# Expert up product: a 512-column and a 256-column matmul in place of three of 256, with the partial sums added outside TensorE

## The reference, cut to what matters

```
u = modulate(x, sh_ffn, sc_ffn)              # 256 x 1024
y = (gelu(u @ U.T) * G) @ V                  # 256 x 1024
x = layer_norm(DN_ALPHA * x + g_ffn * y, ln2_g, ln2_b)
```

## Time and profile before

| | |
|---|---|
| median of 3 runs | 4242.46 us (4237.34 to 4247.29) |
| the profiled execution | 4238.88 us, its span 4237.0 us |
| busy share | PE 81%, PEld 71%, DVE 63%, ACT 43%, POOL 2% |
| TensorE clock granted, mean | 0.908 of full |
| HBM | 633.89 MB read, 150 GB/s over the span |
| expert stages | 796 to 1553 us and 2316 to 3065 us of the span |

### The profile page before, as it was taken

How to read it: one execution, slowest core, us unless ns; L and a number is a source line. 1 busy time by engine, 2 the same in 40 slices (tenths; PEclk the granted TensorE clock), 3 DMA queues, 4 the chain that set the end, 5 groups by cost and what they waited for, 6 DMA issues and landing times. The chain is left out here.

```text
span 4237.0 us, 63766 instructions
## 1 busy us (share of the span) xinstructions
PE 3434.5 (81%) x20020; PEld 2995.3 (71%) x20020; DVE 2650.1 (63%) x5102; ACT 1804.1 (43%) x3292; POOL 80.7 (2%) x66
## 2 busy tenths in 40 slices
PE   4877763899999969778727999999964689795698
PEld 3766653788888859567626888888853579684597
DVE  6764569777777763544588777777544366444465
ACT  2343314755555534333118555555512244343244
POOL 0010000000000000100000000000002100000000
PEclk8988987999999989889869999999976989897899
DMA  6515320377767744134300777776430153550243
GB/s 236 175 28 169 124 90 20 105 238 238 238 238 238 242 154 146 54 115 147 116 25 20 243 238 238 240 241 232 166 104 26 45 191 141 169 188 6 109 159 119
DMA packets 262229, 636.61 MB, mean 150 GB/s; under 512 B 38902, under 2 KB 78338, under 8 KB 255964
## 3 DMA queue, kind: packets, MB, share of 16 engines
q1 hardware_dynamic: 262032, 635.03, 44.1%
q10 hardware_dynamic: 76, 0.08, 0.0%
HBM read 633.89 MB, written 1.15 MB: 150 GB/s over the span
## 5 line engine op out<-in xcount | busy, mean ns | idle before, releaser
L130 PE MATMUL experts_ps_h<-uP_hi,experts_u_hi 128*128 128x256 f32 x2048 | 587.2, 287 | 14.5 <-DVE experts_u_lo L125 14.0
L132 PE MATMUL experts_ps_h<-uP_hi,experts_u_lo 128*128 128x256 f32 x2048 | 581.1, 284 | 0.0
L131 PE MATMUL experts_ps_h<-uP_lo,experts_u_hi 128*128 128x256 f32 x2048 | 581.1, 284 | 0.0
L125 DVE TENSOR_TENSOR experts_u_lo<-u_w,experts_u_hi 128x512 fp32r<-128x512 f32 x512 | 339.9, 689 | 320.1 <-ACT experts_u_hi L122 315.7
L122 ACT ACTIVATE experts_u_hi<-u_w 128x512 fp32r<-128x512 f32 x512 | 310.6, 629 | 504.7 <-DMA u_w<-in_peer_u 391.3
L130 PEld LDWEIGHTS experts_ps_h<-uP_hi,experts_u_hi 128*128 128x128 f32 x2048 | 393.6, 192 | 65.2 <-issue 40.6
L125 DVE TENSOR_TENSOR experts_v_lo<-v_w,experts_v_hi 128x512 fp32r<-128x512 f32 x512 | 353.8, 691 | 103.9 <-ACT experts_v_hi L122 95.9
L130 PE MATMUL expert_y<-experts_v_hi,experts_w_hi 128*128 128x512 f32 x1024 | 402.1, 393 | 3.0 <-DVE experts_w_lo L125 3.0
L131 PE MATMUL expert_y<-experts_v_lo,experts_w_hi 128*128 128x512 f32 x1024 | 401.5, 392 | 0.0
L131 PEld LDWEIGHTS experts_ps_h<-uP_lo,experts_u_hi 128*128 128x128 f32 x2048 | 393.8, 192 | 7.3
L132 PE MATMUL expert_y<-experts_v_hi,experts_w_lo 128*128 128x512 f32 x1024 | 398.3, 389 | 0.0
(11 more groups left out here) (507 smaller groups left out, 7400.5 us busy)
## 6 DMA issues: line engine op xcount, KB each, us to landing
u_w<-in_peer_u SPq DMA_DIRECT2D x256, 512.0 KB, 5.1
v_w<-in_peer_v SPq DMA_DIRECT2D x256, 512.0 KB, 3.9
experts_mod_w<-in_ada_w_all SPq DMA_DIRECT2D x152, 512.0 KB, 4.9
up_w<-in_ffn_w_up SPq DMA_DIRECT2D x44, 1024.0 KB, 6.1
od_in_w<-in_od_w_in SPq DMA_DIRECT2D x36, 1024.0 KB, 5.1
in_w<-in_w_in SPq DMA_DIRECT2D x48, 752.0 KB, 4.5
merge_w_w<-in_w_gate SPq DMA_DIRECT2D x32, 1024.0 KB, 5.1
down_w<-in_ffn_w_down SPq DMA_DIRECT2D x44, 512.0 KB, 3.8
```

The source lines that it names most:

```text
L125: return dve.tensor_tensor(self.lo[at], value, self.hi[at].bitcast(F32), ALU.subtract)
L130: pe.matmul(out, left.hi[left_at], right.hi[right_at], start=start, stop=False, skip_group_check=skip)
L131: pe.matmul(out, left.hi[left_at], right.lo[right_at], start=False, stop=False, skip_group_check=skip)
L132: return pe.matmul(out, left.lo[left_at], right.hi[right_at], start=False, stop=stop, skip_group_check=skip)
```

## The change

`uP` becomes one tile in which high and low activations of a chunk lie side by side. In the up product the expert's high part takes both as one moving operand of 512 columns, and writes hi.hi to the first and hi.lo to the second 256 columns of a PSUM bank; the expert's low part adds lo.hi to the first 256. The two halves are then added outside PE: ACT copies the second half to `experts_low`, DVE adds it to the first half, ACT applies Gelu to that sum, now from SBUF. Sum, Gelu and gated weight share one buffer (`experts_hid`). Two semaphores, `low_done` and `sum_done`, order this.

```diff
--- before.py
+++ after.py
@@ -123,6 +123,14 @@
 
     def write_lo(self, dve, at, value):
         return dve.tensor_tensor(self.lo[at], value, self.hi[at].bitcast(F32), ALU.subtract)
+
+
+class Beside(Parts):
+
+
+    def __init__(self, nc, stack, name, chunks, width):
+        self.both = stack.enter_context(nc.sbuf_tensor(f"{name}_both", [P, chunks, 2, width], FR))
+        self.hi, self.lo = self.both[:, :, 0], self.both[:, :, 1]
 
 
 def split_matmul(pe, out, left, left_at, right, right_at, start, stop, skip=False):
@@ -1474,11 +1482,13 @@
         vp = [Parts(nc, s.stack, f"{name}_v{c}", [P, D // 2]) for c in range(2)]
         wp = [Parts(nc, s.stack, f"{name}_w{v}", [P, T]) for v in range(2)]
         hid = s.sb("hid", [P, T])
-        wgt = s.sb("wgt", [P, T])
+        wgt = pre_h = hid
+        low = s.sb("low", [P, T])
         ps_h = s.ps("ps_h", [P, 2, 512])
         work = SpreadModulation(s, silu, *ada, mods, slotT[0:1, 0:2].rearrange("p a t -> p (a t)"))
         u_hi, u_split, u_used = s.sem("u_hi"), s.sem("u_split"), s.sem("u_used")
         v_hi, v_split, v_used = s.sem("v_hi"), s.sem("v_split"), s.sem("v_used")
+        low_done, sum_done = s.sem("low_done"), s.sem("sum_done")
         gelu_done, gated, w_hi, w_split = s.sem("gelu_done"), s.sem("gated"), s.sem("w_hi"), s.sem("w_split")
         ALL = slice(None)
         units = sum(count for m, _, count in spread if m is not None)
@@ -1524,7 +1534,10 @@
                         pe.wait_ge(u_split, n * 2 + (h + 1))
                         for k in range(HK):
                             kk = h * HK + k
-                            mm = split_matmul(pe, ps_h[:, u % 2, 0:T], up[h], (ALL, k), uP, (ALL, kk), kk == 0, kk == KD - 1)
+                            pe.matmul(ps_h[:, u % 2], up[h].hi[:, k], uP.both[:, kk].rearrange("p a t -> p (a t)"),
+                                      start=kk == 0, stop=False, skip_group_check=True)
+                            mm = pe.matmul(ps_h[:, u % 2, 0:T], up[h].lo[:, k], uP.hi[:, kk], start=False, stop=kk == KD - 1,
+                                           skip_group_check=True)
                         mm.then_inc(u_used, 1)
 
                 def add_up(n, u, start=False, stop=False):
@@ -1562,9 +1575,10 @@
 
                 def tail(n, u, loads):
                     act.wait_ge(u_used, n * 2 + 4)
-                    if not (isinstance(n, int) and n == 0):
-                        act.wait_ge(gated, n)
-                    act.activation(hid[:], ps_h[:, u % 2, 0:T], ACT.Gelu).then_inc(gelu_done, 1)
+                    act.wait_ge(sum_done, n + 1)
+                    act.activation(low[:], ps_h[:, u % 2, T:2 * T], ACT.Copy).then_inc(low_done, 1)
+                    act.wait_ge(sum_done, n + 2)
+                    act.activation(hid[:], pre_h[:], ACT.Gelu).then_inc(gelu_done, 1)
                     act.wait_ge(pre_v.loaded[u], loads * 16)
                     for c in range(2):
                         act.wait_ge(v_used, n * 2 + (c + 1))
@@ -1594,9 +1608,11 @@
                         work.add(dve, unit, m, u)
 
                 def tail(n, u, loads):
-                    dve.wait_ge(gelu_done, n + 3)
+                    dve.wait_ge(low_done, n + 1)
                     if not (isinstance(n, int) and n == 0):
                         dve.wait_ge(w_split, n)
+                    dve.tensor_tensor(pre_h[:], ps_h[:, u % 2, 0:T], low[:], ALU.add).then_inc(sum_done, 1)
+                    dve.wait_ge(gelu_done, n + 3)
                     dve.tensor_tensor(wgt[:], hid[:], table[:, bass.ds(n, 1), :].rearrange("p a t -> p (a t)"),
                                       ALU.mult).then_inc(gated, 1)
                     dve.wait_ge(pre_v.loaded[u], loads * 16)
@@ -1608,6 +1624,7 @@
                             wp[u % 2].write_lo(dve, ALL, wgt[:]).then_inc(w_split, 1)
 
                 work.begin_vector(dve)
+                dve.sem_inc(sum_done, 1)
                 each(dve, step)
                 tail(NKEYS - 1, RING - 1, NKEYS // RING)
 
@@ -2568,7 +2585,7 @@
         g.iota = sb("iota", [P, NKEYS])
         g.silu = sb("silu", [P, 2, KD])
         x = sb("x", [P, TB, D])
-        uP = Parts(nc, stack, "uP", [P, KD, T])
+        uP = Beside(nc, stack, "uP", KD, T)
         load_tiles(nc, "load", [(g.ident[:], a["k_ident"]), (g.iota[:], a["k_iota"]), (x[:], a["x"])])
         first_modulation(nc, "mod0", g, a["c_all"], a["ada_w_all"][0], a["ada_b_all"][0], a["mods"][0])
         for l in range(DEPTH):
```

## The result

| | median us | lowest to highest | ratio to before (95%) |
|---|---|---|---|
| before, same chip | 4243.55 | 4237.34 to 4247.29 | |
| after | 4371.03 | 4366.0 to 4372.67 | 1.0302 (1.0288 to 1.0317) |

The change costs 127.5 us, 3%. It lies outside the predicted range of 4221 to 4262, on the other side of zero. The profiled execution of after took 4366.0 us, its span is 4364.2.

A forecast was written before the change was run, and what follows sets the result against it. PE was taken to bound the kernel, with DVE not far behind. PE -22, lateness +14 and stage starts +1.6 gave -6.4, say -7 on the median of 4242.5: 4235 us, range 4221 to 4262.

The forecast's parts named there:

- PE, -22: Up product: three matmuls per chunk become two, 0.360 to 0.349 us, over 8 chunks x 256 blocks: -22 us.
- Rival C: Up product: the pair doesn't get cheaper, PE gains 5 us or nothing, lateness stays: +6, 4248 us; chance 0.07.
- Prices of the added instructions: ACT and DVE, per block: copy from PSUM 0.366 us, Gelu from SBUF 0.410, sum 0.421.
- The lateness, +14: Loads of u and w_lo: the longer chain makes PE wait more, 0.47 us at the critical places; +14 us together.
- Where PE waits: Steps with late u_hi: whole chain added, adds end 0.95 us later, PE loses about 0.1 us more.
- two critical places per round: Loads of u for steps 2 and 3, behind the adds of steps 0 and 1; 76 in all.
- Every other load of u: Loads of u outside steps 2 and 3: they wait for a v_lo, which ends before the adds, with more cover.
- Rival B: Steps 0 to 3: the DVE-to-load loop decides, each round waits 1 us more: +18, 4260 us; chance 0.23.
- w_lo in the loop: Add-up of late steps: PE waits 0.1 us for w_lo at some 40 waits, 4 us within the +14.
- The start of a stage: First block of each expert stage: nothing hides the chain, PE waits longer for w_lo; +1.6 us for two stages.

The follow-up runs named there:

- padded pair: Changed kernel without copy and sum (Gelu reads the first half of the bank), plus 224 one-column matmuls in the first modulation: 4231.7 us, 0.9971.
- padded kernel: Changed kernel, whole, plus 224 one-column matmuls in the first modulation that change no data: 4328.5 us, 1.0194.
- e1: Changed kernel with its up product again three matmuls of 256 columns per chunk; copy, sum and Gelu stay: 4327.1 us, 1.0207.
- e1 padded: e1 plus 224 one-column matmuls in the first modulation: 4312.9 us, 1.0165.
- e10: Kernel before plus one idle DVE addition of 0.42 us in front of the gate product: 4247.8 us, 1.0018.
- e11: Kernel before plus two idle DVE additions, 0.84 us, in front of the gate product: 4276.4 us, 1.0091.

## Why the prediction was wrong

**PE, -22: right in direction, too large.** In time it appears only where PE decides: 13 us between the two kernels with u first (4219.9 and 4232.9; 11 by their ratios), 10 between the padded pair and before. The starts in these two kernels, changed and before, show where the rest is (first matmul of an up product, of the add-up, of the next up product):

```profile
1127.22 0.39 PE L1537 MATMUL experts_ps_h<-uP_both,experts_u_hi 128*128 128x512 f32 x1
1130.03 0.40 PE L138 MATMUL expert_y<-experts_v_hi,experts_w_hi 128*128 128x512 f32 x1
1132.81 0.39 PE L1537 MATMUL experts_ps_h<-uP_both,experts_u_hi 128*128 128x512 f32 x1
```

```profile
1129.94 0.28 PE L130 MATMUL experts_ps_h<-uP_hi,experts_u_hi 128*128 128x256 f32 x1
1132.81 0.40 PE L130 MATMUL expert_y<-experts_v_hi,experts_w_hi 128*128 128x512 f32 x1
1135.56 0.28 PE L130 MATMUL experts_ps_h<-uP_hi,experts_u_hi 128*128 128x256 f32 x1
```

The up product went from 2.87 to 2.81 us, 0.352 a chunk, worth 15 us over 256 blocks. The add-up behind it, whose instructions did not change, went from 2.75 to 2.78, which takes 8 us back. So the block gained 0.03 us and not 0.09; why the add-up got longer no run shows. The rule of the Trainium skill (TensorE: Matmul & The Clock Gate, Back-to-back issue gap) gives 0.325 us for the pair by an estimate from its formula, which it states for an isolated matmul; the pair took 0.352, so the trace does not agree. Rival C was wrong that the up product would stay at 2.87 us, but its -5 is nearer to these 7 us than my -22.

**Prices of the added instructions: right.** Gelu 418 ns, copy 364, sum 418. The estimate from the Trainium skill (VectorE: DVE Perf Modes, the TRN2 errata) of 0.065 us more for a source in PSUM is not borne out: the gate product, from SBUF alone, takes 426.

**The lateness, +14: wrong, and the failed step.** I had both halves in hand and joined them wrongly. "Where PE waits" says that the adds end 0.95 us later in a step whose u_hi came late; the timeline after has 6.46 where I had 6.38. But the sum took 0.47 us, from the rows of a block in which nothing was late, for all 76 places, and called the 0.95 harmless: "The later adds of such a step 2 or 3 gate the bias and pieces of a later unit, which have cover." They have none. With 5.71 us per step against PE's 5.59, DVE is late after the adds of step 3 and still so in step 4: it ends that step's v_lo at 1110.01, SP's load of v waits for it, and behind that in SP's queue stand the piece and u of place 0 (1110.19, 1111.71, 1112.39 in the round shown). The adds of that place gate place 2 again. So there were not two critical places per round but a closed loop. "Every other load of u ... has more cover" failed by the same fact: at places 0 and 1 the slack of 1.5 and 1.8 us is down to 0.2. What I never computed was DVE's own step with the new gap in it, to set beside PE's. Measured, this term is 87 us by the padded kernel (4328.5 against 4241.6), 87 by e1 and 71 by e1 padded, where I had 14. The 87 of the padded kernel is after PE's gain of some 10, so there the loop costs near 100.

**Rival B: right in mechanism, wrong in size.** It named adds, SP, load of u for steps 2 and 3, and the traces show that chain. I gave it 0.23, because PE rarely waited, and priced it at 1 us a round, +18 in all, since it too used the chain of an undisturbed block. With the late block's chain the loop is 6.46 + 0.17 + 0.68 + 5.99 = 13.30 for two steps against 11.18, and that is 2.1 of the 3.5 us a round that the first stage lost. Few waits before did not mean a long way to the edge: e10 and e11 show that 0.42 us are nearly free and 0.84 are not.

**Duration of the transfers: not foreseen.** I let every load keep its time from before. Those of u took 5.7 in place of 5.1 us, the pieces 5.5 in place of 4.9. Worth 43 us by the padded kernel, some of it not explained by the durations, as e1 shows. With the 87 above it makes 129.4; less the 1.9 by which the kernel before differs between the two chips, that is the whole loss of 127.5.

**w_lo in the loop:** predicted some 40 waits, there are 142, 37 us. But e1 has 4 of them and loses 87 us all the same, so most of the loss does not need them. Whether they make up the 16 us between the two padded kernels was not separated.

The start of a stage (+1.6) wasn't isolated. Left open is what padding changes; a kernel with padding of other sizes or only in code outside TensorE was not run.

**The best version** is the changed kernel with the load of u first: 4219.9 us, 0.5% faster than before.

## What to carry to other kernels

Work out the step of every in-order engine as if it were late, its new waits included, and set it beside the step of the engine that bounds: where it is longer, lateness is carried from step to step, and a mean busy share of 71% says nothing of it. It costs nothing as long as there is slack to carry it in, as with u first. When an edit lengthens the chain on such an engine, look at what an in-order DMA queue holds behind it; here moving one load ahead of one wait was worth more than the edit itself. And a margin that is nearly used up has a convex price: test it by adding dummy work of known length before building the real thing.

## What the runs showed that I had not expected

- The same 512 KB transfer took a median of 4.7 to 4.9 or of 5.3 to 5.5 us (pieces), and 5.0 to 5.2 or 5.4 to 5.7 (u), in kernels that issue the same DMAs in the same order, and unrelated instructions in another stage brought the short durations back in the two kernels with the pair. Of the other loads issued 16 times or more only one moved by over 0.3 us between before and after, `in_w`, from 4.5 to 5.0, and padding left it at 5.0.
- Put first in SP's queue, u takes 4.7 to 4.9 us and the piece behind it 5.3 to 5.7; put second, u takes 5.0 to 5.7 and the piece 4.7 to 5.5. v has 3.3 to 4.0 in all kernels.
- A pair of 512 and 256 columns of fp32r with different weights repeats every 0.352 us on average, close to the sum of the two distances measured apart (0.229 + 0.120), and an unchanged add-up behind it takes 2.78 us in place of 2.75.
